# Delta-rule mixer: block-diagonal matrices of two 64-token blocks kept as 128x64 per head, products as 64x64 quarters

## The reference

```
    decay = jnp.exp(jnp.where(incl, gc[..., :, None] - gc[..., None, :], -jnp.inf))
    kb = kc * bc[..., None]
    vb = vc * bc[..., None]
    a_low = jnp.where(strict, jnp.einsum('bhncd,bhnsd->bhncs', kb, kc) * decay, 0.0)
    t_inv = lax.linalg.triangular_solve(a_low + eye, jnp.broadcast_to(eye, a_low.shape), ...)
    u = jnp.einsum('bhncs,bhnse->bhnce', t_inv, vb)
    w = jnp.einsum('bhncs,bhnsd->bhncd', t_inv, kb * jnp.exp(gc)[..., None])
    qk = jnp.einsum('bhncd,bhnsd->bhncs', qc, kc) * decay
```

## Time and profile before

| | |
|---|---|
| median of 3 runs | 2198.69 us |
| the profiled execution, its own time | 2197.22 us |
| its span, first to last instruction | 2195.4 us |
| TensorE busy (matmuls) | 97% of the span |
| VectorE, ScalarE, GpSimd busy | 71%, 59%, 4% |
| even mixer in the span | about 1246 to 1460 us |
| its attention with the levels | about 1354 to 1400 us |

### The profile page before, as it was taken

One profiled execution on the slowest core, in us unless ns is written; L12 is line 12 of the kernel. 1 busy time (PEld: TensorE's weight loads), 2 busy tenths in 40 slices (PEclk: granted clock), 3 DMA queues, 4 the chain that ended last, 5 costly groups with the idle time before them and its releaser, 6 DMA issues.

```text
span 2195.4 us, 33169 instructions
## 1 busy us (share of the span) xinstructions
PE 2134.9 (97%) x12373; PEld 1834.1 (84%) x12373; DVE 1563.5 (71%) x2774; ACT 1295.3 (59%) x2162; POOL 77.1 (4%) x46
## 2 busy tenths in 40 slices
PE   8999999999999999999999998999999999999998
PEld 7888978888888967888788896878887888978887
DVE  6777877767767486766777766577666776858676
ACT  6665765556555276655665566446555655666554
POOL 0001000000002200000000001000000000000001
PEclk9999999999999999999999999999999999999999
DMA  6454345554544432555455331135544554435552
GB/s 267 179 197 152 140 164 202 187 188 173 200 177 151 160 144 78 201 178 206 148 198 198 141 128 39 59 136 211 191 158 173 201 201 145 158 126 187 193 195 84
DMA packets 64954, 362.97 MB, mean 165 GB/s; under 512 B 7512, under 2 KB 8280, under 8 KB 32792
## 3 DMA queue, kind: packets, MB, share of 16 engines
q1 hardware_dynamic: 64368, 360.31, 44.9%
q0 software_dynamic: 128, 0.26, 0.0%
q10 hardware_dynamic: 296, 0.27, 0.0%
HBM read 359.77 MB, written 1.05 MB: 164 GB/s over the span
## 4 chain that ended last, share of the span: by engine, by line
PE 81%; DVE 11%; ACT 6%; issue 1%; DMA 0%; POOL 0%; DVEq 0%; ACTq 0%; SPq 0%; POOLq 0%
PE ps L202 80%; DVE WL L120 4%; ACT work L192 2%; ACT WH L192 2%; PE ps L207 2%; DVE work L120 2%; ACT XBt L192 1%; DVE XBt L131 1%; DVE work L131 1%; DVE small L120 1%; DVE small L131 1%; DVE work L157 0%; DVE work L125 0%; ACT L192 0%; DVE small L127 0%
## 5 line engine op out<-in xcount | busy, mean ns | idle before, releaser
L202 PE MATMUL ps<-XBt,WH 128*128 128x512 f32 (+1 forms) x4208 | 1214.0, 355 | 16.4 <-DVE WL L120 6.8
L120 DVE TENSOR_TENSOR WL<-ring,WH 128x1024 fp32r<-128x1024 f32 (+1 forms) x642 | 790.7, 1232 | 369.7 <-ACT WH L192 325.4
L192 ACT ACTIVATE WH<-ring 128x1024 fp32r<-128x1024 f32 (+1 forms) x662 | 701.3, 1059 | 356.3 <-PE ps L202 294.7
L202 PE MATMUL ps<-XBt,WL 128*128 128x256 f32 x3384 | 896.4, 280 | 0.0
L202 PEld LDWEIGHTS ps<-XBt,WH 128*128 128x128 f32 x4208 | 730.3, 190 | 124.8 <-DVE XBt L131 13.2
L202 PEld LDWEIGHTS ps<-XBt,WL 128*128 128x128 f32 x3384 | 642.2, 190 | 26.2
L202 PE MATMUL ps<-WH,HHt 128*128 128x512 f32 x712 | 279.3, 392 | 1.0 <-DVE WL L120 0.7
L202 PE MATMUL ps<-WL,HHt 128*128 128x512 f32 x712 | 277.2, 389 | 0.0
L202 PE MATMUL ps<-WH,HLt 128*128 128x512 f32 x712 | 274.6, 389 | 0.0
L192 ACT ACTIVATE work<-ps 128x256 f32<-128x256 f32 (+5 forms) x454 | 186.2, 414 | 76.6 <-PE ps L202 38.7
L192 ACT ACTIVATE work<-work 128x256 f32<-128x256 f32 (+6 forms) x222 | 98.8, 445 | 177.9 <-DVE work L120 174.3
(11 more groups left out here) (134 smaller groups left out, 1199.1 us busy)
## 6 DMA issues: line engine op xcount, KB each, us to landing
ring<-wts SPq DMA_DIRECT2D x248, 1024.0 KB, 5.8
ring<-wts SPq DMA_DIRECT2D x179, 512.0 KB, 3.7
ring<-wts SPq DMA_DIRECT2D x1, 1152.0 KB, 5.1
ct<-cons SPq DMA_DIRECT2D x1, 1086.5 KB, 5.6
Xt<-x SPq DMA_DIRECT2D x4, 256.0 KB, 5.4
out<-Xt SPq DMA_DIRECT2D x4, 256.0 KB, 2.0
work<-wts SPq DMA_DIRECT2D x1, 512.0 KB, 5.5
ring<-wts SPq DMA_DIRECT2D x1, 288.0 KB, 6.1
```

Source lines behind the costliest of these rows:

```text
L120: self.done(self.e and self.e.tensor_tensor(out, a, b, op), inc)
L192: self.done(self.e and self.e.activation(out, a, f, **kw), inc)
L202: inst = self.e and self.e.matmul(out, l, r, start=start, stop=stop)
```

## The change

Each matrix of tokens by tokens loses its zero blocks: block e of head h stands on partitions 64e to 64e+63 in columns 64h to 64h+63, so that a group's matrix is 128x256. A product of four heads becomes eight products of 64x64 blocks, each on 64 rows and 64 columns of the array; the two of a head lie on opposite quarters of the array and write opposite partition halves of one bank. The transposes of level 0 become products with the identity. Products with values keep 128 streamed columns (64*64 64x128); products with keys have 64 rows and 128 columns of weights (64*128 64x64), and write two banks, one per block. Masks, identity and triangle in the new form are made by three additions on GpSimd at the stage's start. Elementwise work on the matrices has 256 columns instead of 512, or 64 per head instead of 128; the copy of the key products (`WT`) becomes two of 256 columns per group. `chunk_pe` reads the new places; its shapes stay.

```diff
+            def blocks_pe(P, use, end, f, *needs):
+                ps.take(use)
+                P.wait_ge(*needs, *ps.free(use))
+                for h in range(4):
+                    for e in range(2):
+                        r = slice(64 * e, 64 * e + 64)
+                        left, right = f(h, e, r, slice(64 * h, 64 * h + 64))
+                        P.mm(ps[use][r, 64 * h:64 * h + 64], left, right, True, True, inc=use if h == 3 and e else None)
+                ps.give(use, end)
+            def blocks_cast_pe(P, use, D, i, end, *needs):
+                blocks_pe(P, use, end, lambda h, e, r, c: (con("mask4")[0:4, h * 128 + 64 * e:h * 128 + 64 * e + 64],
+                                                           D[:, i * 128 + 64 * e:i * 128 + 64 * e + 64]), *needs)
...
-                    cast_pe(P, f"ev.g{i}", R[0][:, hs(i)], f"ev.gx{i}", "ev.r2")
+                    blocks_cast_pe(P, f"ev.g{i}", R[0], i, f"ev.gx{i}", "ev.r2")
...
+                blocks_pe(P, f"ev.k2{i}", f"ev.at{i}", lambda h, e, r, c: (tok(K3, h, e), tok(K3, h, e)))
+                blocks_pe(P, f"ev.qk{i}", f"ev.qkm{i}", lambda h, e, r, c: (tok(K3, h, e), tok(Q3, h, e)), "ev_gq.0.si", "ev_gq.1.si")
...
-                cast_pe(P, f"ev.b{i}", R[1][:, hs(i)], f"ev.b{i}.e", "ev.r1")
+                blocks_cast_pe(P, f"ev.b{i}", R[1], i, f"ev.b{i}.e", "ev.r1")
                 cast_pe(P, f"ev.e{i}", R[2][:, hs(i)], f"ev.qg{i}", "ev.r2")
...
-                        four_pe(P, f"ev.am0{i}", f"ev.tt1{i}", lambda o, h, inc: P.tr(o, AM[i][:, hs(h)], IDN, inc), f"ev.lv0{i}")
+                        blocks_pe(P, f"ev.am0{i}", f"ev.tt1{i}", lambda h, e, r, c: (AM[i][r, c], IDN[r, r]), f"ev.lv0{i}")
...
+                        blocks_pe(P, f"ev.xu{lv}{i}", f"ev.ut{lv + 1}{i}", lambda h, e, r, c: (XB4[i][r, c], U[i][r, c]),
+                                  f"ev.xx{lv}{i}", f"ev.ut{lv}{i}")
+            def solved_pe(P, i):
+                for use in (f"ev.uv{i}", f"ev.kw{i}0", f"ev.kw{i}1"):
+                    ps.take(use)
...
+                        P.mm(ps[f"ev.uv{i}"][r, hs(h)], U[i][r, c], VB[i][r, hs(h)], True, True, inc=f"ev.uv{i}" if h == 3 and e else None)
...
+                        P.mm(ps[f"ev.kw{i}{e}"][:, c], KBG[i][r, hs(h)], U[i][r, c], True, True, inc=f"ev.kw{i}{e}" if h == 3 else None)
...
-                    A.act(XX[i], ps[f"ev.am{lv}{i}"], ACT.Copy, inc=f"ev.xx{lv}{i}")
+                    A.act(XB4[i], ps[f"ev.am{lv}{i}"][:, 0:256], ACT.Copy, inc=f"ev.xx{lv}{i}")
...
-                    A.act(WT[i], ps[f"ev.kw{i}"], ACT.Copy, inc=f"ev.wt{i}")
+                    for e in range(2):
+                        A.wait_ge(f"ev.kw{i}{e}")
+                        A.act(WT[i][:, e * 256:e * 256 + 256], ps[f"ev.kw{i}{e}"][:, 0:256], ACT.Copy, inc=f"ev.wt{i}{e}", back=1 + e)
...
-                        V.tt(T[i], T[i], ps[f"ev.ux{lv}{i}"], SUB, inc=f"ev.tt{lv + 1}{i}")
+                        V.tt(TB4[i], TB4[i], ps[f"ev.ux{lv}{i}"][:, 0:256], SUB, inc=f"ev.tt{lv + 1}{i}")
...
+                G_.tt(LEV, v3(con("lev"), 6)[:, :, 0:64], v3(con("lev"), 6)[:, :, 64:128], ADD)
+                G_.tt(BD, bdT[:, 0:64], bdT[:, 64:128], ADD, back=2)
+                G_.tt(ID, IDN[:, 0:64], IDN[:, 64:128], ADD, inc="ev.blocks", back=3)
...
-                        G_.tt(v3(AM[i], 4), v3(ATm[i], 4), over(lev[:, lv * 128:lv * 128 + 128], 4, 128), MUL, inc=f"ev.lv{lv}{i}")
+                        G_.tt(v3(AM[i], 4), v3(ATm[i], 4), over(LEV[:, lv, :], 4, 64), MUL, inc=f"ev.lv{lv}{i}")
```

More of the change, by code:

```diff
@@ L1968, in even_mixer @@
             Q3, K3, V3 = v3(at(7168, 1024), 4), v3(at(14336, 1024), 4), v3(at(15360, 1024), 4)
-            KBG, VB, KD, ATm, QKM, XX = [two_(8192 + 1024 * k) for k in range(6)]
-            U, T, AM = [two_(14336 + 1024 * k) for k in range(3)]
+            KBG, VB, KD, XX, T = [two_(a) for a in (8192, 9216, 10240, 13312, 15360)]
+            ATm, QKM, XB4, U, TB4, AM = [[at(a + 512 * i, 256) if a != 11264 else at(a + 256 * i, 256) for i in range(2)]
+                                         for a in (11264, 12288, 13312, 14336, 15360, 16384)]
+            LEV, BD, ID = v3(at(11776, 384), 6), at(12160, 64), at(12224, 64)
             WT, S_ = two_(2048), at(3072, 512)
@@ new lines, in level_pe @@
+                        blocks_pe(P, f"ev.xu{lv}{i}", f"ev.ut{lv + 1}{i}", lambda h, e, r, c: (XB4[i][r, c], U[i][r, c]),
+                                  f"ev.xx{lv}{i}", f"ev.ut{lv}{i}")
+            def solved_pe(P, i):
+                for use in (f"ev.uv{i}", f"ev.kw{i}0", f"ev.kw{i}1"):
+                    ps.take(use)
+                P.wait_ge(f"ev.ut6{i}", f"ev.ve{i}", *ps.free(f"ev.uv{i}"))
+                for h in range(4):
+                    for e in range(2):
+                        r, c = slice(64 * e, 64 * e + 64), slice(64 * h, 64 * h + 64)
+                        P.mm(ps[f"ev.uv{i}"][r, hs(h)], U[i][r, c], VB[i][r, hs(h)], True, True, inc=f"ev.uv{i}" if h == 3 and e else None)
+                P.wait_ge(f"ev.ke{i}", *ps.free(f"ev.kw{i}0"), *ps.free(f"ev.kw{i}1"))
+                for h in range(4):
+                    for e in range(2):
+                        r, c = slice(64 * e, 64 * e + 64), slice(64 * h, 64 * h + 64)
+                        P.mm(ps[f"ev.kw{i}{e}"][:, c], KBG[i][r, hs(h)], U[i][r, c], True, True, inc=f"ev.kw{i}{e}" if h == 3 else None)
+                ps.give(f"ev.uv{i}", f"ev.uu{i}")
+                for e in range(2):
+                    ps.give(f"ev.kw{i}{e}", f"ev.wt{i}{e}")
@@ L2142, in chunk_pe @@
                 r = slice(64 * e, 64 * e + 64)
-                half = lambda h: slice(h * 128 + 64 * e, h * 128 + 64 * e + 64)
+                block = lambda h: slice(h * 64, h * 64 + 64)
                 if not e:
@@ L2148, in chunk_pe @@
                     ps.take(use)
[L2149 removed]
+                    P.wait_ge(f"ev.wt{i}{e}", f"ev.st{n - 1}", *ps.free(use))
                     for h in range(4):
[L2151 removed]
+                        P.mm(ps[use][r, hs(h)], WT[i][:, e * 256 + h * 64:e * 256 + h * 64 + 64], S_[:, hs(h)], True, True, inc=use if h == 3 else None)
                     ps.give(use, f"ev.vn{n}")
@@ L2407, in act @@
                 for i in range(2):
-                    A.wait_ge(f"ev.kw{i}")
-                    A.act(WT[i], ps[f"ev.kw{i}"], ACT.Copy, inc=f"ev.wt{i}")
+                    for e in range(2):
+                        A.wait_ge(f"ev.kw{i}{e}")
+                        A.act(WT[i][:, e * 256:e * 256 + 256], ps[f"ev.kw{i}{e}"][:, 0:256], ACT.Copy, inc=f"ev.wt{i}{e}", back=1 + e)
                 hi(A, ahead("ev_z.0"))
@@ L2566, in dve @@
                 for i in range(2):
-                    V.wait_ge(f"ev.xe{i}")
+                    V.wait_ge(f"ev.xe{i}", "ev.blocks")
                     for h in range(4):
-                        V.stt(XX[i][:, hs(h)], XX[i][:, hs(h)], RK[:, i * 4 + h:i * 4 + h + 1], bdT, MUL, MUL, back=4 if h else 1)
+                        c = slice(64 * h, 64 * h + 64)
+                        V.stt(XB4[i][:, c], XB4[i][:, c], RK[:, i * 4 + h:i * 4 + h + 1], BD, MUL, MUL, back=4 if h else 1)
                 taps_dve(V, "ev_gv.1")
```

42 lines of the change are left out of this document (16 added, 26 removed).

## The result

The changed kernel takes 2185.47 us (median, 2184.43 to 2187.36) against 2198.67 for the kernel before: a ratio of 0.9938, 95% interval 0.9926 to 0.995. That is 13.2 us less; 2186.0 was forecast. In a later group of runs the same kernel gave 2186.19 us; that median counts one slow run of 7425.72 us, and the other four have 2185.9.

The account below looks back on a forecast made before the run. TensorE, busy 97% of the span, was taken as the bound. Attention 11.2 plus 2.25 before it minus 0.8 behind it gives 12.6 us: 2198.69 - 12.6 = 2186.0 us, range 2181 to 2191, with (a) to 2194.

Parts of the forecast that it names:

- The unit: Set of four heads' products for one group: 8 pairs at 0.0585 us, 0.47 instead of 0.89, saving 0.42.
- rows 5: Earlier trace rows: 64-column halves of one bank, same rows, start two at a time, a pair every 0.06 us.
- (b): Rival: a head's two quarters don't run at once because they write one bank from different rows; 2203.7 us, chance 0.09.
- (c): Rival: quarters take turns at 0.109 us, a set takes 1.74, the kernel 2231 us; chance 0.05.
- Changes of shape: Switching the array's product shape on TensorE costs 0.2 us back to 128 columns, 0.14 to 64 columns.
- The attention: Scores to gate: 26 sets save 11.0, the start 1.5, shape changes cost 1.3; 11.2 us gained, period 7.3.
- The chain: Attention path through VectorE and ScalarE after a level's last second product: 4.35 us, TensorE asks at 4.6; 0.2 slack.
- (a): Rival: the chain of other engines binds in the attention, giving back 5 to 5.5 us; 2191.5 us, chance 0.15.
- Before the attention: Products ahead of the scores: `decay_pe` saves 0.9 and `inner_pe` 1.35, 2.25 us in all.
- projections and ScalarE's copies behind them are TensorE-paced: Reason ahead of the attention for counting the savings of `decay_pe` and `inner_pe` in full, 2.25 us.
- The stretch at the lower clock: Risk to the size: one more stretch at 1.2 GHz in the attention costs 2 to 3 us, one fewer gains that.

Follow-up runs that it names:

- The run on one quarter: Changed kernel with both 64x64 products of each head made on the same quarter of the array (result not the reference's): 2199.08 us, ratio 1.0007 to the kernel before.
- the later weight pieces: Changed kernel with VectorE forming the next weight matrix's four pieces in steps 3, 5, 7, 9 instead of 2, 4, 6, 8: 2183.08 us, ratio 0.9936.
- the wide run: Changed kernel with the level work's copies, subtractions and masks back at 512 columns a group, products still 64x64: 2189.58 us, ratio 0.9955.
- The repeated decay: Changed kernel with the products of the decay matrix, and the inner products, issued twice with the same result: 2188.08 us, ratio 0.9949.
- the rounding moved forward: Changed kernel with later weight pieces and reordered value/key products, plus ScalarE's rounding for the second value projection ahead of the latent queries: 2183.86 us, ratio 0.9931.

## Why the prediction was right

**The unit.** Forecast were a pair of quarters every 0.0585 us and a set of 0.47; measured are 0.058 and 0.47. The value from rows 5 held, and with it the whole forecast. Rivals (b) and (c) had their premise refuted: pairs start together in one bank, and turns at 0.109 don't occur. The run on one quarter, 2199.08, shows about what (b) would have brought. (b)'s own sum, 2203.7, has 1.7 for the products with values, which still pair in that run; the remaining 2202.0 is 2.9 us above the measured time, and why is open.

**Changes of shape.** Taken at 0.2 and 0.14. Around the products with values and keys 0.8 was expected, and the second gate half starts 0.76 us later than before, counted from the first. Two changes less gave 0.30.

**The attention.** 11.2 expected, 11.9 measured. Its first part gave 1.8 instead of 1.5, though both of its steps were met (group 0 at 1357.06 and group 1 at 1358.20, forecast 1357.2 and 1358.4; this attention began 0.16 sooner). The period is 6.99 to 7.41 instead of 7.3, and the whole 34.1 instead of "near 35". With the later weight pieces, where the waits are gone, it is 7.04: by the records, the 9.54 that the forecast started from held about 0.2 us of waiting, which it took for work. A mask is 0.74 us, where 0.7 was taken.

**The chain.** "It just holds, with 0.2 of slack" was right in that rival (a) did not come, but there was no slack: TensorE starts 0.1 to 0.2 us late in the steps (from the transposes at 1365.94 to the next products are 0.67 us, at 1370.17 they are 0.43), and once waits 0.56 for VectorE at head 8. The later weight pieces, which remove these waits, gain 1.2 us. The path was counted too kindly. I put one subtraction, 0.27, on it; the wide run shows that four queue on VectorE once sets are 0.47 apart. The narrow subtractions, 0.42, just keep up with the sets. Without the narrow elementwise work the attention would have lost 3.2 us, more than half of case (a).

**Before the attention.** 2.25 expected, 1.8 measured. `inner_pe` won 1.56, of which 0.2 went into the change of shape, as the step says (1.35). What failed is "projections and ScalarE's copies behind them are TensorE-paced" for the decay's 0.9. Behind it the second value projection waits for weights that VectorE forms after a rounding on ScalarE, which stands behind the latent queries in ScalarE's list. And the clock, which the step left out, changes what each part costs: with a wait of 1.44 us inside the stretch at half clock, the column sums are 1.34 shorter and the projection 0.67 longer, and about 0.3 of the 0.9 are kept. The repeated decay shows the same from the other side (0.35 of 0.93), and the rounding moved forward shows that the wait alone is worth no more than 0.4. In return 0.13 more came ahead of the scores.

**The execution.** The profiled one showed 11.2 of 12.9 us, since it met the lower clock in other places. The traces give 12.9 where 12.6 was forecast: the attention was put 0.7 too low and what stands ahead of it 0.45 too high. That these two cancel for the most part is luck. The median moved by 13.2; the rest is within what the runs scatter. The stretch at the lower clock that the prediction priced at 2 to 3 us cost 1.6 where one came, in the wide run.

## What to carry to other kernels

If a matrix is block diagonal, don't count only the zeros saved: ask whether the two small products land on opposite parts of the array, and issue them alternately, or in turns of at most four passes, the longest turn that still paired here. When products get shorter, look at the queue of elementwise operations behind them: a subtraction of 0.42 us behind sets 0.47 us apart stayed hidden, one of 0.67 us made four of them queue, and then all of the queue counts. Judge such an edit by distances between the same instructions in two traces, from a point behind all that is unchanged, and look whether a stretch at the lower clock lies between them; whole times move by as much with the clock.

## What the runs showed of the hardware

- Two 64x64 products on opposite quarters run at once into opposite partition halves of one bank (0.058 us a pair with 64 columns), and so do two half arrays (128*64 128x64, 64 passes in 2.01 us).
- Products on opposite quarters pair fully in turns of two passes (0.47 us a set of 16) and of four (0.48), and only in part in turns of eight (0.62 to 0.66). By the records, a pass for the other quarter starts with up to three passes ahead of it not yet begun.
- In both kernels a stretch at the lower clock (1.2 GHz) begins in the column sums (one column a product) that follow the decay's four-row products. A wait that falls into it costs less than its length: 1.06 us of waiting removed gave 0.4.
- The nsa mixer, unchanged, ran at a mean granted clock of 0.64 in one profiled execution and at 0.82 to 0.88 in the others, from 758 to 786 us; that one came out of it over 5 us behind the kernel before.
